# Modulation by direct fp32 products on four column tiles, and a new order of the first panels

## The chip, the cores and the metric

The kernel runs on one core of a Trainium2 chip. The metric is the device time of one execution in microseconds (us), from the first to the last instruction with what lies around them. Five engines work side by side and meet at semaphores: TensorE (PE), whose weight loads are listed as PEld, VectorE (DVE), ScalarE (ACT), GpSimd (POOL) and SyncE (SP), which here only issues DMA transfers.

## The reference, cut to what matters

Two transformer blocks run one after the other on 256 tokens of width 1024, in fp32. The change lies at the start of the first one:

```
mod = silu(c) @ w_ada + b_ada              # 1024 x 6144, in six parts: sh1, sc1, gt1, sh2, sc2, gt2
mod_c = silu(c_ctx) @ w_ada + b_ada        # the same for the context
h  = rmsnorm(x, g_norm1)   * (1 + sc1)  + sh1      # 256 x 1024
hc = rmsnorm(ctx, g_norm1) * (1 + scc1) + shc1     # 256 x 1024
cq, ckv, kpe, rq, rk, rv, rg       = split(h  @ w_in)   # 256 256 32 512 512 512 512 columns
_, ckv_c, kpe_c, _, rk_c, rv_c, _  = split(hc @ w_in)
q = rmsnorm(cq, g_q) @ w_uq                # latent attention's queries
... retention over rq, rk, rv with states from rk_c, rv_c, gated by silu(rg) ...
```

So nothing of `h` can be formed before sh1 and sc1 are there: the first 2048 columns of w_ada, 8 MB. The context needs only four of the seven panels of w_in.

## The kernel before, in words

**Units.** All weights come as units of 512 KB or less (128 partitions x 1024 fp32 values; mostly two slices of 128 rows of a panel of 512 columns). SP issues their DMAs in the order of one list, into six buffers `raw`, and waits before each for the release of the unit six places earlier. ACT then rounds a unit to `w_hi` (L1527), DVE forms the rest `w_lo` = raw - w_hi (L2093), into three buffers each, and PE makes a product as three in fp32r: hi x hi, lo x hi, hi x lo (`three`, L742 to L744). ACT may round a unit only when PE is through with the unit three places earlier.

**Names.** ada0 to ada3 are the first four panels of w_ada (shift: ada0, ada1; scale: ada2, ada3), each of four units. cq (two units of 4 slices), rq, ckvpe, rk, rv, rg (four units each) are panels of w_in, uq and ukv those of w_uq and w_ukv. Only ckvpe, rk and rv are multiplied with the context too. ada4 to ada11 are not PE's: DVE sums them itself from `raw` (L2060, L2066: "summed units", two instructions for each unit), and they stand in the list between other units as the table SUMS_BESIDE says.

**Order.** Each engine runs a list of its own that is written out by hand; nothing is reordered. `next(cq)` on PE is one unit of cq, `run(cq)` the rest. Transposes (`turn`, L884) of normalised rows go to a PSUM bank; ACT and DVE turn it into hT_hi and hT_lo (for x1 and ctx with gain and shift through `fbuf`; for mem, cq, ckv and ckvc by L1578/L1580 and L2157). `turn_before` makes a product wait for the pair of slices that it reads. The helper `feed_units(n)` on ACT and on DVE is what issues roundings and rests in the list's order; DVE's `feed_units(fed[0] + 1)`, ahead of the turn of mem among other places, issues exactly one more unit, whatever it is. `feed("rv")` issues up to two units past the last of rv, of which the second last buffer and the last become free only as rv's products end.

**ada0 to ada3 before.** `c_parts` holds silu(c) and silu(c_ctx) in four groups of 32 equal columns (hi and lo of each). Every slice takes two matmuls of 512 columns (L916, L917), with w_hi and w_lo. `ada_spread` (L946) takes the row of results back to columns, from which DVE makes shift and gain (L2198 to L2208). `keep_busy` (L754) are transposes of the identity with no use but to occupy PE.

Of the kernel before, what the change touches and what calls it, by code (L numbers as in the profile page):

```python
# [22 lines left out]
ALU = mybir.AluOpType  # L23
# [33 lines left out]
C_ONES = C_SEL + 2  # L57
# [16 lines left out]
def constants():  # L74
# [4 lines left out]
    c[[0, 32], C_SEL] = 1  # L79
    c[[64, 96], C_SEL + 1] = 1  # L80
# [46 lines left out]
for _g, _vs in enumerate(VEC_GROUPS):  # L127
    _at = 0
    for _name, _n in _vs:
# [7 lines left out]
SUMS_BESIDE = {**{(name, n): 1 for name in ("rv", "rg") for n in range(4)}, ("ukv1", 0): 14,  # L137
# [4 lines left out]
EARLIER = {"cq": (("cq", 0), ("rq", 0), ("rq", 1)),  # L142
           "wout2_0": (("wv1", 0), ("wv1", 1)),
           "wo0": (("wo0", 0), ("wo0", 1), ("wo1", 0))}


def plan_panels(a):
# [10 lines left out]
    def ada(ps):  # L158
        for p in ps:
            add(f"ada{p}", "sum" if p in SUMMED else "ada", a["w_ada"], 512 * p, 512)  # L160

    ada(range(4))
# [69 lines left out]
ADA_ORDER = [0, 1, 2, 3]  # L232


# [40 lines left out]
BUSY = {"score": 8, "start": 17, "spread": 8, "ada": 3,  "ffnpre": 14, "gu0": 8}  # L275
# [10 lines left out]
def build(nc, a, const, out):  # L286
    panels = plan_panels(a)
    units, units_of, summed = [], {name: [] for name, *_ in panels}, []

    def add_unit(name, k0, nk, cols, sources, kind):  # L290
        units_of[name].append(len(units))
        units.append((name, k0, nk, cols, sources))
        summed.append(kind == "sum")

    sums = [(name, k0, nk, cols, sources, kind) for p in SUMMED for name, kind, kt, nk, cols, sources in panels
            if name == f"ada{p}" for k0 in range(0, kt, nk)]
    for name, kind, kt, nk, cols, sources in panels:
        if kind == "sum":
            continue
        for other, n in EARLIER.get(name, ()):  # L300
            _, kind_, _, nk_, cols_, sources_ = next(x for x in panels if x[0] == other)
            add_unit(other, n * nk_, nk_, cols_, sources_, kind_)
        for n, k0 in enumerate(LATE_FIRST.get(name, range(0, kt, nk))):
            if any((name, n) in early for early in EARLIER.values()):
# [8 lines left out]
    split_units = [u for u in range(len(units)) if not summed[u]]  # L313
    split_of = {u: n for n, u in enumerate(split_units)}
    ends = set(last_unit.values())
    inner = np.cumsum([u not in ends and not summed[u] for u in range(len(units))]).tolist()
# [5 lines left out]
    with ExitStack() as ctx:  # L322
# [22 lines left out]
        c_parts = sb("c_parts", [P, KD, P], F32R)  # L345
        at[0] = c_parts_at
        late_sum = sb("late_sum", [P, 2, 512])
        assert at[0] == c_parts_at + 4 * KD * P
        csilu = sb("csilu", [P, 2, KD])
        modrow = sb("modrow", [P, 2, 512])  # L350
# [16 lines left out]
        cqT_hi = sb("cqT_hi", [P, 2, TOK], F32R)  # L367
        cqT_lo = sb("cqT_lo", [P, 2, TOK], F32R)
# [92 lines left out]
        junk = sb("junk", [P, D])  # L461
        fbuf = sb("fbuf", [P, 2, 2, TOK])
        k0 = sb("k0", [P, C_RCOS])
        ident = k0[:, C_ID:C_ID + P]
        sel_col = k0[:, C_SEL:C_SEL + 2]
# [63 lines left out]
        c_hi_ready = sem("c_hi_ready")  # L529
        c_lo_ready = sem("c_lo_ready")  # L530
# [90 lines left out]

        def gate_of(p):
            return gate[:, p // 8, 512 * (p % 2):512 * (p % 2) + 512]
# [87 lines left out]
        landed = {}  # L711

# [4 lines left out]
        def _(pe):  # L717
# [38 lines left out]
            def panel(name, outs, step, before=None):  # L756
# [6 lines left out]
                for u in units_of[name]:  # L763
                    if tail and u == tail[0]:
                        continue
                    if tail and u == tail[1]:
                        for v in tail:
                            pe.wait_ge(unit_ready, v + 1)
# [13 lines left out]
                    pe.wait_ge(unit_ready, u + 1)  # L782
# [70 lines left out]
            def turn(name, wait_src=None, pairs=None, banks=None):  # L853
# [8 lines left out]
                if name in UNSCALED:  # L862
                    ps_ = list(pairs or range(kt // 2))
                    for p in ps_:
                        claim(("turn", name, p), banks[p % 2] if banks else next_small())
# [12 lines left out]
                for p in pairs or range(kt // 2):  # L878
                    use = ("turn", name, p)
                    o = claim(use, banks[p % 2] if banks else next_small())  # L880
# [28 lines left out]
            turn_vectors(0)  # L909

            def ada_steps(p):
                name = f"ada{p}"
                use = (name, 0)

                def step(k, use, hi, lo, first, last):
                    pe.matmul(ps(use)[:, :], c_parts[:, k, :], hi, start=first, stop=False)  # L916
                    return pe.matmul(ps(use)[:, :], c_parts[:, k, :], lo, start=False, stop=last)  # L917

                yield from panel(name, [use], step)

            def ada(p):
                run(ada_steps(p))

            def sum_spread(p, b=None):
# [4 lines left out]
                pe.wait_ge(unit_ready, last_unit[f"ada{p}"] + 1)  # L929
# [7 lines left out]
            def ada_spread(p, b=None):  # L937

                use = ("spread", p)
                o = claim(use, next_small() if b is None else b)  # L940
                if p == 3:
                    keep_busy(o[:, P:2 * P], BUSY["spread"])
                emptied(pe, (f"ada{p}", 0))
                m = modrow[:, p % 2, :]
                for j in range(4):
                    ins = pe.matmul(o[:, 2 * j:2 * j + 2], m[:, j * P:(j + 1) * P], sel_col, start=True, stop=True)  # L946
                fill(ins, use)

            for p in range(4):
                claim((f"ada{p}", 0), p)  # L950
            keep_busy(ps(("ada3", 0))[:, 0:P], BUSY["start"])
            pe.wait_ge(c_lo_ready, 2)

            def chunk_unit(chunk):

                next(chunk)
                keep_busy(ps(("ada3", 0))[:, 0:P], BUSY["ada"])

            chunk = ada_steps(0)
            for _ in range(4):  # L960
                chunk_unit(chunk)
            run(chunk)
            chunk = ada_steps(1)
            chunk_unit(chunk)
            chunk_unit(chunk)
            turn_vectors(1)
            next(chunk)
            pe.wait_ge(in_sel, 16)
            ada_spread(0, 0)
            run(chunk)  # L970
            chunk = ada_steps(2)
            next(chunk)
            next(chunk)
            ada_spread(1, 1)
            next(chunk)
            turn("x1", None, range(2))
            run(chunk)
            chunk = ada_steps(3)
            next(chunk)
            turn("x1", None, range(2, 4))  # L980
            ada_spread(2, 2)
            run(chunk)
# [5 lines left out]
            ada_spread(3, 7)  # L988
            next(cq)
            next(rq)  # L990
            next(rq)
            run(cq)
            turn("ctx")
# [26 lines left out]
            rows_panel("uq0", cqT_hi, cqT_lo, turn_before("cq"))  # L1020

# [421 lines left out]
        def _(sp):  # L1443
            count = [0] * NRAW
            sp.dma_start(ident, const[:, C_ID:C_ID + P]).then_inc(in_ident, 16)
            for u, (name, k0, nk, cols, sources) in enumerate(units):
                slot = u % NRAW
                if u >= NRAW:

                    sp.wait_ge(unit_ready, u - NRAW + 1)  # L1450
                dst = unit_view(raw[slot], u).rearrange("p (k n) -> p k n", k=nk)
                for c0, width, matrix, m0 in sources:
                    src = matrix[k0 * P:(k0 + nk) * P, m0:m0 + width].rearrange("(k p) n -> p k n", p=P)
                    sp.dma_start(dst[:, :, c0:c0 + width], src).then_inc(raw_landed[slot], 16)
                    count[slot] += 16
                landed[u] = count[slot]
                for group, done, at_unit in ((1, in_vec, NRAW - 1), (2, in_conv, first_unit["rq"] + 2),
                                             (3, in_conv, first_unit["rq"] + 2)):
# [4 lines left out]
                for t in range(T):  # L1463
                    if u == (4, 6)[t]:
                        sp.dma_start(res[:, t, :], a["x"][t * P:(t + 1) * P, :]).then_inc(in_x[t], 16)
                if u == first_unit["rq"]:
# [20 lines left out]
        def _(pool):  # L1487
            pool.memset(mhalf[:, :], -0.5).then_inc(mhalf_ready, 1)
# [10 lines left out]
        def _(act):  # L1499
# [16 lines left out]
            def feed_units(stop):  # L1516

                while fed[0] < min(stop, len(units)):
                    u = fed[0]
                    fed[0] += 1  # L1520
                    if summed[u]:
# [8 lines left out]
            def feed_one(stop=None):  # L1530

                n = fed[0]
                while summed[n]:
# [73 lines left out]
            emptied(act, ("vec", 0))  # L1607
            act.activation(csilu[:, 0, :], vec("c"), ACT.Silu).then_inc(csilu_ready, 1)
# [1217 lines left out]
```

## Time and profile before

| | us |
|---|---|
| median of three executions | 848.87 (848.33 to 849.84) |
| profiled execution | 849.23 |
| its span | 847.4 |
| PE busy | 827.3 (98%) |
| PE weight loads busy | 721.5 (85%) |
| DVE busy | 588.7 (69%) |
| ACT busy | 467.9 (55%) |
| moved by DMA | 152.86 MB, 180 GB/s on average |

PE is busy nearly all the time, so the end moves with what PE has to do and with the time in which it waits. The averages hide the start: there the DMA queues are full and PE waits or runs transposes of no use. A row of a timeline reads: start, duration, engine, line, operation, output <- inputs, shapes, count, and in brackets the idle time of that engine just before and what ended it. Matmuls are pipelined: the shown duration of one is longer than the distance to the next, and a stretch of work is counted from start to start.

### The profile page before, as it was taken

The numbers are of one execution on the slowest core, as the hardware profiler recorded it, in microseconds if no ns is written. First come the engines' busy times: TensorE is split into PE (matmuls) and PEld (weight loads), VectorE is DVE, ScalarE is ACT, GpSimd is POOL, SyncE is SP. The second block draws the span as 40 slices with busy tenths as digits, with TensorE's granted clock in tenths as the row PEclk, the third lists the DMA queues.
The fourth block names the chain that finished last, engine by engine and source line by source line (L and its number), as shares of the span: only waits on it lengthen the run. The fifth ranks groups of instructions, "written<-read, shape, count | busy, mean of one in ns | idle before, by whom it ended". The sixth has DMA issues, their size and how long they took to land. (4 is left out here: it accounts for less than half of the span.)

```text
span 847.4 us, 12808 instructions
## 1 busy us (share of the span) xinstructions
PE 827.3 (98%) x4919; PEld 721.5 (85%) x4919; DVE 588.7 (69%) x919; ACT 467.9 (55%) x757; POOL 16.9 (2%) x24
## 2 busy tenths in 40 slices
PE   6999999999999999999999999999999999999996
PEld 5798888877899999988889978888978788888885
DVE  5885978788777777897767677577457655555444
ACT  6866364366356665663556684556545654444442
POOL 1001000000000000000000000010000000000000
PEclk9999999999999999999999999999999999999999
DMA  9973573165656656669758642254504656565551
GB/s 331 373 245 100 172 227 112 50 199 170 210 176 192 195 179 180 178 213 313 238 149 302 195 153 101 75 174 149 174 26 150 195 178 198 179 188 180 190 158 50
DMA packets 103668, 152.86 MB, mean 180 GB/s; under 512 B 6538, under 2 KB 55862, under 8 KB 103608
## 3 DMA queue, kind: packets, MB, share of 16 engines
q1 hardware_dynamic: 102296, 149.21, 55.6%
q10 hardware_dynamic: 1312, 2.83, 0.9%
q8 instruction: 39, 0.64, 0.3%
q14 instruction: 21, 0.17, 0.1%
HBM read 150.97 MB, written 1.05 MB: 179 GB/s over the span
## 5 line engine op out<-in xcount | busy, mean ns | idle before, releaser
L2093 DVE TENSOR_TENSOR w_lo<-raw,w_hi 128x1024 fp32r<-128x1024 f32 (+1 forms) x244 | 294.5, 1212 | 147.1 <-ACT w_hi L1527 146.2
L1527 ACT ACTIVATE w_hi<-raw 128x1024 fp32r<-128x1024 f32 (+1 forms) x244 | 254.5, 1050 | 197.4 <-PE bank L744 138.6
L742 PE MATMUL bank<-w_hi,hT_hi 128*128 128x512 f32 (+2 forms) x400 | 156.2, 390 | 1.2 <-DVE w_lo L2093 0.6
L744 PE MATMUL bank<-w_hi,hT_lo 128*128 128x512 f32 (+2 forms) x400 | 152.9, 382 | 0.0
L743 PE MATMUL bank<-w_lo,hT_hi 128*128 128x512 f32 (+2 forms) x400 | 152.7, 382 | 0.0
L845 PE MATMUL bank<-hT_hi,w_hi 128*128 128x256 f32 x512 | 145.1, 283 | 0.0
L847 PE MATMUL bank<-hT_hi,w_lo 128*128 128x256 f32 x512 | 145.0, 283 | 0.0
L846 PE MATMUL bank<-hT_lo,w_hi 128*128 128x256 f32 x512 | 145.0, 283 | 0.0
L846 PEld LDWEIGHTS bank<-hT_lo,w_hi 128*128 128x128 f32 x512 | 96.8, 189 | 0.0
L847 PEld LDWEIGHTS bank<-hT_hi,w_lo 128*128 128x128 f32 x512 | 96.8, 189 | 0.0
L845 PEld LDWEIGHTS bank<-hT_hi,w_hi 128*128 128x128 f32 x512 | 96.8, 189 | 0.0
L742 PEld LDWEIGHTS bank<-w_hi,hT_hi 128*128 128x128 f32 x400 | 75.2, 188 | 16.7 <-DVE w_lo L2093 2.3
L744 PEld LDWEIGHTS bank<-w_hi,hT_lo 128*128 128x128 f32 x400 | 75.1, 188 | 15.0
L743 PEld LDWEIGHTS bank<-w_lo,hT_hi 128*128 128x128 f32 x400 | 75.3, 188 | 13.4
L742 PE MATMUL bank<-w_hi,act_hi 128*128 128x512 f32 x176 | 69.7, 396 | 0.4 <-DVE w_lo L2093 0.3
L744 PE MATMUL bank<-w_hi,act_lo 128*128 128x512 f32 x176 | 68.5, 389 | 0.0
L743 PE MATMUL bank<-w_lo,act_hi 128*128 128x512 f32 x176 | 68.5, 389 | 0.0
L742 PEld LDWEIGHTS bank<-w_hi,act_hi 128*128 128x128 f32 x176 | 33.0, 188 | 8.5 <-DVE w_lo L2093 1.5
L743 PEld LDWEIGHTS bank<-w_lo,act_hi 128*128 128x128 f32 x176 | 33.0, 188 | 7.2 <-issue 0.5
L744 PEld LDWEIGHTS bank<-w_hi,act_lo 128*128 128x128 f32 x176 | 33.0, 188 | 7.0
L1495 POOL TENSOR_TENSOR rstd<-var,mhalf 128x2 f32<-128x2 f32 (+3 forms) x18 | 14.8, 823 | 825.1 <-DVE var L2752 254.7
L1143 PEld LDWEIGHTS bank<-k,prob 128*128 128x128 f32 x104 | 12.6, 140 | 14.7 <-ACT probT L1807 8.0
(346 smaller groups left out, 1196.6 us busy)
## 6 DMA issues: line engine op xcount, KB each, us to landing
raw<-w_up_dram SPq DMA_DIRECT2D x132, 256.0 KB, 3.4
raw<-w_ada_dram SPq DMA_DIRECT2D x48, 512.0 KB, 4.8
raw<-w_down_dram SPq DMA_DIRECT2D x44, 512.0 KB, 4.3
raw<-w_in_dram SPq DMA_DIRECT2D x40, 512.0 KB, 4.6
raw<-w_gate_dram SPq DMA_DIRECT2D x44, 256.0 KB, 2.9
raw<-w_out_dram SPq DMA_DIRECT2D x16, 512.0 KB, 3.4
raw<-wk_x_dram SPq DMA_DIRECT2D x8, 512.0 KB, 4.7
raw<-wv_x_dram SPq DMA_DIRECT2D x8, 512.0 KB, 3.4
```

Of the source, the lines that this page charges most:

```text
L742: pe.matmul(o, xh, yh, start=first, stop=False, skip_group_check=skip)
L743: pe.matmul(o, xh, yl, start=False, stop=False, skip_group_check=skip)
L744: return pe.matmul(o, xl, yh, start=False, stop=last, skip_group_check=skip)
L845: pe.matmul(o, hi[:, c:c + P], xh[:, k, :], start=f, stop=False, skip_group_check=True)
L846: pe.matmul(o, hi[:, c:c + P], xl[:, k, :], start=False, stop=False, skip_group_check=True)
L847: ins = pe.matmul(o, lo[:, c:c + P], xh[:, k, :], start=False, stop=last, skip_group_check=True)
L1143: ins = pe.transpose(o[:, j * P:(j + 1) * P], prob_of(i)[:, j * P:(j + 1) * P], ident)
L1495: pool.tensor_tensor(rstd[:, r, c:w], var[:, r, c:w], mhalf[:, c:w], ALU.pow).then_inc(rstd_ready, 1)
L1527: act.activation(unit_view(w_hi[n % NSPLIT], u), unit_view(raw[u % NRAW], u), ACT.Copy).then_inc(w_hi_ready, 1)
L2093: dve.tensor_tensor(unit_view(w_lo[n % NSPLIT], u), unit_view(raw[u % NRAW], u), unit_view(w_hi[n % NSPLIT], u).bitcast(F32), ALU.subtract ...
```

## The change

Four things change.

1. **ada0 to ada3 are multiplied directly from `raw`**, in plain fp32, with no rounding by ACT and no rest by DVE. `c_cols` holds silu(c) and silu(c_ctx) as two of 32 columns (the others are zero). A unit (2 slices x 512 columns) is four matmuls of 32 x 256, one for each slice and half, written to partitions 0, 32, 64 and 96 of a bank; `ada_spread` adds the slices (2 matmuls where there were 4).
2. **The list of units** begins ada0, ada2; then ada1 and ada3 stand among units of cq, rq and rg. x is loaded behind units 1 and 3, the context behind the third unit of rg.
3. **PE multiplies ten units of cq, rq and rg** with x before it turns to ckvpe, the first panel with the context; before there were six (cq, rq), and rg followed rv. The turn of cq stands ahead of the last unit of rv, and uq0 directly behind rv; ckv and ckvc are turned after uq0. silu(rg) is taken by ACT between the turns of the context, where the table that holds silu is still loaded.
4. **The summed units** stand beside rk 1 to 3, rv 0 to 3 and uq0, where they stood beside rv 0 to 3 and rg 0 to 3. `feed_units` on DVE is as it was.

```diff
-SUMS_BESIDE = {**{(name, n): 1 for name in ("rv", "rg") for n in range(4)}, ("ukv1", 0): 14,
+SUMS_BESIDE = {**{(name, n): 1 for name in ("rk", "rv") for n in range(4) if name == "rv" or n},
+               ("uq0", 0): 1, ("ukv1", 0): 14,
...
-EARLIER = {"cq": (("cq", 0), ("rq", 0), ("rq", 1)),
+EARLIER = {("ada1", 0): (("cq", 0),), ("ada1", 1): (("rq", 0),), ("ada1", 2): (("rq", 1),),
+           ("ada3", 2): (("rg", 0),), ("cq", 1): (("rg", 1), ("rq", 2), ("rg", 2)), ("rq", 3): (("rg", 3),),
...
-BUSY = {"score": 8, "start": 17, "spread": 8, "ada": 3,  "ffnpre": 14, "gu0": 8}
+BUSY = {"score": 8, "start": 24, "spread": 8, "ada": 4, "ffnpre": 14, "gu0": 8}
...
+            def direct_unit(u):
+                name, k0, nk, cols, _ = units[u]
+                use = (name, 0)
+                pe.wait_ge(raw_landed[u % NRAW], landed[u])
+                w = unit_view(raw[u % NRAW], u).rearrange("p (k n) -> p k n", k=nk)
+                for kk in range(nk):
+                    for half in range(2):
+                        j = 32 * (2 * kk + half)
+                        ins = pe.matmul(ps(use)[j:j + 32, 0:TOK], c_cols[:, k0 + kk, :],
+                                        w[:, kk, half * TOK:(half + 1) * TOK],
+                                        start=u == first_unit[name], stop=u == last_unit[name])
...
             next(cq)
+            direct_unit(units_of["ada1"][1])
             next(rq)
+            for u in units_of["ada1"][2:]:
+                direct_unit(u)
             next(rq)
+            ada_spread(1, 6)
+            for u in units_of["ada3"]:
+                direct_unit(u)
+            next(rg)
+            ada_spread(3, 6)
+            turn("x1", None, range(2, 3), (7,))
+            next(rg)
+            turn("x1", None, range(3, 4), (6,))
+            next(rq)
+            next(rg)
             run(cq)
-            turn("ctx")
+            run(rg)
+            turn("ctx", None, None, (6, 7, 0, 1))
             run(rq)
...
-            rows_panel("rv", hT_hi, hT_lo, None, cT, b=4)
-            rg = rows_steps("rg", hT_hi, hT_lo, b=2)
-            next(rg)
-            next(rg)
-            for name in ("cq", "ckv", "ckvc"):
-                turn(name)
-            run(rg)
+            rv = rows_steps("rv", hT_hi, hT_lo, None, cT, b=4)
+            for _ in range(3):
+                next(rv)
+            turn("cq", None, None, (0,))
+            run(rv)
+            rows_panel("uq0", cqT_hi, cqT_lo, turn_before("cq"))
+            turn("ckv", None, None, (2,))
+            turn("ckvc", None, None, (3,))
```

The three places below show what stands in a row on an engine (line numbers of the changed kernel differ by some ten).

DVE around the turn of mem, which PE makes behind the third of rk's four units. Before (memT_lo is what DVE makes of the turned rows, kpe_row the rows that it worked on ahead of it):

```order
L2242 TENSOR_TENSOR kpe_row<-rtmp 128x2x8
L2093 TENSOR_TENSOR w_lo_54<-raw_137,w_hi_51 128x1024
L2157 SCALAR_TENSOR_TENSOR memT_lo<-bank,vcol_145,memT_hi 128x256 x8
L2093 TENSOR_TENSOR w_lo_52<-raw_132,w_hi_49 128x1024
L2066 SCALAR_TENSOR_TENSOR modrow<-raw_133,csilu,gate 128x512
```

The same place now:

```order
L2244 TENSOR_TENSOR kpe_row<-rtmp 128x2x8
L2069 SCALAR_TENSOR_TENSOR modrow<-raw_134,csilu,modrow 128x512 x2
L2168 SCALAR_TENSOR_TENSOR memT_lo<-bank,vcol_145,memT_hi 128x256 x8
L2104 TENSOR_TENSOR w_lo_54<-raw_135,w_hi_51 128x1024
L2069 SCALAR_TENSOR_TENSOR modrow<-raw_130,csilu,modrow 128x512 x2
```

The unit that `feed_units(fed[0] + 1)` issues ahead of the turn was the rest of rk's fourth unit; now it is a summed unit, and the rest of rk's fourth unit follows behind memT_lo.

ACT at the end of rv. Before (the last row with w_hi_49 is the unit that waits for the end of rv's products):

```order
L1527 ACTIVATE w_hi_49<-raw_132 128x1024
L1705 ACTIVATE rv_row<-bank 128x512 x2
L1705 ACTIVATE rvc_row<-bank 128x512 x2
L1708 ACTIVATE decay<-decay 128x512 x4
L1527 ACTIVATE w_hi_50<-raw_134 128x1024
L1715 ACTIVATE xi_f<-k_63,lgam 128x256
```

The same place now:

```order
L1539 ACTIVATE w_hi_51<-raw_135 128x768
L1539 ACTIVATE w_hi_49<-raw_130 128x1024
L1590 ACTIVATE cqT_hi<-bank,vcol_145 128x256
L1592 ACTIVATE cqT_hi<-bank,vcol_145 128x256
L1723 ACTIVATE rv_row<-bank 128x512 x2
L1723 ACTIVATE rvc_row<-bank 128x512 x2
L1726 ACTIVATE decay<-decay 128x512 x4
L1590 ACTIVATE ckvT_hi<-bank,vcol_145 128x256
```

cqT_hi stands now directly behind the rounding that waits for rv's end (it is a unit of ukv0); on DVE the rest of that unit stands ahead of cqT_lo likewise.

PE from the last unit of ada2 to the first product with x, now (raw_131 is ada2's last unit, raw_133 ada1's first):

```order
L894 MATMUL bank<-k_143,row 128x128 x4
L928 MATMUL bank<-raw_131,c_cols 32x256 x4
L894 MATMUL bank<-k_143,row 128x128 x4
L955 MATMUL bank<-k_143,modrow 128x4 x2
L764 MATMUL bank<-k_143 128x128 x8
L928 MATMUL bank<-raw_133,c_cols 32x256 x4
L764 MATMUL bank<-k_143 128x128 x8
L752 MATMUL bank<-w_hi_49,hT_hi 128x256
```

Before, all sixteen units of ada0 to ada3 stood ahead of the first product with x; now nine do.

## Rows read from the trace of the kernel before

**Rows 1.** The page's slices 1 to 40: granted clock (tenths), PE busy.

```profile
PE   6999999999999999999999999999999999999996
PEclk9999999999999999999999999999999999999999
```

**Rows 2.** Windows: length, busy of PE PEld DVE ACT POOL, clock, DMA share, GB/s.

```profile
30.00:40.00 10.00, 10.00 (x70) 8.71 (x69) 8.45 (x16) 8.12 (x12) 0.00 (x0) 1.00 1.02 371
24.00:26.00 2.00, 1.84 (x5) 1.28 (x5) 1.93 (x5) 1.69 (x3) 0.00 (x0) 0.50 1.05 387
26.00:28.00 2.00, 2.00 (x13) 1.81 (x12) 1.48 (x4) 1.06 (x1) 0.00 (x0) 0.85 1.00 365
```

**Rows 3.** Timeline of the start: ada1's last unit lands, a wait, to the first product.

```profile
18.28 1.06 ACT L1527 ACTIVATE w_hi<-raw 128x1024 fp32r<-128x1024 f32 x1 [0.97 <-DMA raw<-w_ada_dram]
22.63 0.51 PE L916 MATMUL bank<-w_hi,c_parts 128*128 128x512 f32 x1 [0.79 <-DVE w_lo L2093]
33.57 1.02 ACT L1597 ACTIVATE fbuf<-bank,modc,acol 128x256 f32<-128x256 f32 x2 [0.81 <-DVE acol L2208]
35.57 1.23 DVE L2093 TENSOR_TENSOR w_lo<-raw,w_hi 128x1024 fp32r<-128x1024 f32 x1
37.64 0.36 PE L742 MATMUL bank<-w_hi,hT_hi 128*128 128x256 f32 x1
```

**Rows 4.** Timeline of PE: a unit of cq, one of rg, plain fp32, start of ckvpe.

```profile
46.39 0.28 PE L742 MATMUL bank<-w_hi,hT_hi 128*128 128x256 f32 x1
49.27 1.91 PE L884 MATMUL bank<-k,in_ctx 128*128 128x128 f32 x16
56.59 0.38 PE L742 MATMUL bank<-w_hi,hT_hi 128*128 128x288 f32 x1
114.81 0.39 PE L742 MATMUL bank<-w_hi,hT_hi 128*128 128x512 f32 x1
117.53 0.39 PE L742 MATMUL bank<-w_hi,hT_hi 128*128 128x512 f32 x1
135.35 3.62 PE L1041 MATMUL bank<-rqT,rkT 128*128 128x256 f32 x16
```

**Rows 5.** Timeline of ACT: ckvpe's first rounding, behind the turn of ctx; silu(rg).

```profile
52.30 0.68 ACT L1527 ACTIVATE w_hi<-raw 128x576 fp32r<-128x576 f32 x1
131.16 1.08 ACT L1730 ACTIVATE sgate<-bank 128x512 f32<-128x512 f32 x2
```

**Rows 6.** Timeline at the turn of mem.

```profile
86.06 1.23 DVE L2093 TENSOR_TENSOR w_lo<-raw,w_hi 128x1024 fp32r<-128x1024 f32 x1
87.40 3.23 DVE L2157 SCALAR_TENSOR_TENSOR memT_lo<-bank,vcol,memT_hi 128x256 fp32r<-128x256 f32 x8
87.50 0.48 PE L742 MATMUL bank<-w_hi,hT_hi 128*128 128x512 f32 x1
```

**Rows 7.** Timeline behind rv: ACT, DVE, then PE to the states.

```profile
115.07 1.06 ACT L1527 ACTIVATE w_hi<-raw 128x1024 fp32r<-128x1024 f32 x1 [4.38 <-PE bank L744]
116.16 1.23 DVE L2093 TENSOR_TENSOR w_lo<-raw,w_hi 128x1024 fp32r<-128x1024 f32 x1 [1.26 <-ACT w_hi L1527]
117.94 2.21 ACT L1708 ACTIVATE decay<-decay 128x512 f32<-128x512 f32 x4
124.17 0.47 ACT L1578 ACTIVATE cqT_hi<-bank,vcol 128x256 fp32r<-128x256 f32 x1
125.03 0.87 DVE L2157 SCALAR_TENSOR_TENSOR cqT_lo<-bank,vcol,cqT_hi 128x256 fp32r<-128x256 f32 x2 [1.10 <-ACT cqT_hi L1580]
130.94 1.28 DVE L2354 COPY rkT<-bank 128x512 f32<-128x512 f32 x2
129.27 0.41 PE L742 MATMUL bank<-w_hi,cqT_hi 128*128 128x384 f32 x1 [0.32 <-DVE w_lo L2093]
131.67 0.60 PE L1030 MATMUL bank<-rvc_row,rkf 128*128 128x128 f32 x3
```

**Rows 8.** Timeline of PE: its longest wait behind the start.

```profile
503.08 0.33 PE L1143 MATMUL bank<-k,prob 128*128 128x128 f32 x1 [1.46 <-ACT probT L1807]
```

More of the change, by code:

```diff
@@ L159, in ada @@
         for p in ps:
-            add(f"ada{p}", "sum" if p in SUMMED else "ada", a["w_ada"], 512 * p, 512)
-    ada(range(4))
+            add(f"ada{p}", "sum" if p in SUMMED else "direct", a["w_ada"], 512 * p, 512)
+    ada((0, 2, 1, 3))
     add("cq", "rows", a["w_in"], 0, 256, nk=4)
@@ L287, in build @@
     panels = plan_panels(a)
-    units, units_of, summed = [], {name: [] for name, *_ in panels}, []
+    units, units_of, summed, direct = [], {name: [] for name, *_ in panels}, [], []
     def add_unit(name, k0, nk, cols, sources, kind):
@@ L947, in ada_spread @@
                 fill(ins, use)
[L949 to L964, printed above, removed]
@@ L965, in _ @@
-            chunk_unit(chunk)
-            turn_vectors(1)
-            next(chunk)
-            pe.wait_ge(in_sel, 16)
[L969 to L980, printed above, removed]
+            turn_vectors(0, 4)
@@ new lines, in _ @@
+            for p, b in ((0, 0), (2, 1), (1, 6), (3, 7)):
+                claim((f"ada{p}", 0), b)
+            idle = ps(("ada3", 0))[:, 0:P]
+            keep_busy(idle, BUSY["start"])
+            pe.wait_ge(csilu_ready, 3)
+            for u in units_of["ada0"]:
+                direct_unit(u)
+                keep_busy(idle, BUSY["ada"])
+            turn_vectors(1, 2)
+            pe.wait_ge(in_sel, 16)
+            ada_spread(0, 3)
+            for u in units_of["ada2"][:3]:
+                direct_unit(u)
+                keep_busy(idle, BUSY["ada"])
@@ L981, in _ @@
+            turn("x1", None, range(1), (4,))
+            direct_unit(last_unit["ada2"])
+            turn("x1", None, range(1, 2), (5,))
             ada_spread(2, 2)
-            run(chunk)
+            keep_busy(idle, BUSY["spread"])
+            direct_unit(units_of["ada1"][0])
+            keep_busy(idle, BUSY["spread"])
             cT = (hcT_hi, hcT_lo)
@@ L1448, in _ @@
                 if u >= NRAW:
-                    sp.wait_ge(unit_ready, u - NRAW + 1)
+                    v = u - NRAW
+                    if not direct[v]:
+                        sp.wait_ge(unit_ready, by_dve[v])
+                    elif v in ends:
+                        ready(sp, (units[v][0], 0))
+                    else:
+                        sp.wait_ge(direct_used, inner_direct[v])
                 dst = unit_view(raw[slot], u).rearrange("p (k n) -> p k n", k=nk)
@@ L1532, in feed_one @@
                 n = fed[0]
-                while summed[n]:
+                while summed[n] or direct[n]:
                     n += 1
@@ L1659, in _ @@
             turn("ctx", None, range(2))
-            feed_units(last_unit["rq"] + 2)
+            for t in range(T):
+                use = ("rg", t)
+                ready(act, use)
+                free(act.activation(sgate[:, t, :], ps(use)[:, :], ACT.Silu), use)
+            feed_units(first_unit["ckvpe"] + 1)
             full("ctx", 3)
```

224 lines of the change are left out of this document (105 added, 119 removed).

## The prediction

> **What bounds the kernel now.** I read the slices of the page first: PE is 90% busy or more in all but the first and the last [rows 1], so a change pays only by what it takes from PE or from PE's waits. Then the windows of the start: the DMA queues are full (share about 1.0, 371 to 387 GB/s), while VectorE (DVE) and ScalarE (ACT) are busy 8 tenths of the time with halves of weights [rows 2]. Then the timeline: w_ada's eighth unit, the tenth transfer of 512 KB, is rounded the moment it lands, at 18.28 us, but the first product with x starts only at 37.64 [rows 3]. Until then PE does nothing but modulation, transposes and filler. From there to the attention it hardly waits. So the start is worth up to 15 us, and each new wait behind it costs its full length. Last I read, at the places that the order of instructions names, what PE does at each moment and who releases it [rows 4 to 8].
>
> **The change part by part.** All sums are made in the profiled execution's time, 849.23 us (span 847.4); the median shown is 0.36 lower, and I take that off at the end.
>
> *The start.* With 387 GB/s [rows 2] a unit of 512 KB lands every 1.35 us. In the new list ada2's last unit is again the tenth such transfer: 18.25. Its product, ACT's copy, the spread and the gain are worth some 2.1 us. Before, the chain from the gain's first user on ACT (33.57) to the first product (37.64) took 4.1 us [rows 3], of which about 1 us was hT_lo waiting behind a weight's rest on DVE (35.57, 1.23 us); 3.0 to 3.5 are left, so the first product starts at about 23.4, 14 us earlier. But seven units of ada1 and ada3 are still to come. The last one is the 22nd transfer, 12 behind the tenth: 18.25 + 12 x 1.35 = 34.5. PE's way there: one unit of cq (46.39 to 49.27: 2.88 us), two of rq (114.81 to 117.53: 2.72 each [rows 4]), a spread, and six direct units: 23.4 + 8.7 + six direct units, 33.5 to 34.5 if one takes 0.2 to 0.4. So DMA sets this point.
>
> What a direct unit costs no row shows. From above: a plain fp32 product of 256 columns takes (3.62 - 0.38)/15 = 0.216 us start to start [rows 4], where 0.38 is the pipelined duration of the last; four in a row 0.86. From below: all four at once, 0.22. I take 0.4 (two by two), since the four write to different partitions and have no operand in common but c_cols; at anything up to that the sum stays with DMA. The Trainium skill (TensorE: Matmul & The Clock Gate, Part 3: Packing small matmuls) says that matmuls whose outputs lie at partitions 32j run concurrently; no row here shows it, and by that rule the unit would be 0.2 to 0.3 and the time below the same within 0.2 us.
>
> So ada3 is through at 35.0. Behind it PE has six units of rg and rq (16.3), one of cq (2.9), a spread and two short turns (1.3), the turn of ctx (49.27 to 50.93, 1.7) and two vector transposes (0.1): ckvpe could start at 57.3. Before it started at 56.59 [rows 4], with rg's four units (10.9) still ahead: like with like, 67.5. Gain 10.2.
>
> *Waits in it.* rq's third unit waits about 0.6 for DVE, which makes spread, gain and hT_lo of pair 2 first. At the turn of ctx ACT rounded ckvpe's first unit 3.0 us behind the turn's start, at 52.30, and PE needed it at 56.59. Now ACT takes silu(rg) first, 1.08 [rows 5], and only one unit of rq (2.72) instead of two covers: w_lo comes at turn + 5.5, PE is there at turn + 4.7. (Rounding 0.68, its rest about as much.) With the same delay once more at ckvpe's second unit, and a bit at the fourth, 1.7. The start is left with 10.2 - 0.6 - 1.7 = 7.9.
>
> *The turn of mem.* DVE's helper issues one unit ahead of it. That was rk's fourth rest, made in 86.06 to 87.29, just in time for PE's 87.50 [rows 6]. Now that unit is a summed one, and the rest comes behind memT_lo. The summed unit ends at about 87.6; memT_lo takes 3.23, or until 90.9; the rest 1.23: 92.1. PE, through with its transposes at 87.5, waits **4.6 us**. Nothing covers it: everything on PE is queued behind this product. DVE reaches the place no sooner than before, since decay and k_pe ahead of it hang on the end of ckvpe, as PE's own three units of rk do.
>
> *The query latent.* Its transposes lie inside rv, but on ACT cqT_hi is queued behind the rounding that waits for rv's last product: 115.07 in the trace, and DVE's rest of that unit is 116.16 to 117.39 [rows 7]. cqT_hi takes 0.86 (124.17 to 125.03), so it is ready by 117.0; cqT_lo then goes to 117.4 + 0.87 = 118.2. uq0 could have started at 114.81: **3.4 us**. Before, rg's units lay there. After uq0 (2.4) come 24 transposes (2.6) to 123.3, and the retention's states need a bank that DVE frees with rkT. ACT does the copies of rv and exp(decay) first (some 4.1 us: before, from the rounding's end to 117.94 + 2.21), then ckvT_hi, DVE ckvT_lo and the copy: 124.3. **1.0 us** more. The wait of 0.32 before uq0 goes [rows 7]. Sum 4.1.
>
> *Hidden at nothing:* 16 roundings and 16 rests less in the first 35 us, where DMA bounds; and the summed units, which lie beside products of rk and rv. Should DVE lose its lead there, a product of rv would wait for its rest, by the length of one summed unit.
>
> *Sum:* 849.2 - 7.9 + 4.6 + 4.1 = 850.0.
>
> *The clock.* After short waits on PE, the last of 0.79 us before 22.63 [rows 3], the granted clock fell to half (0.50 in 24 to 26, 0.85 in 26 to 28) and stayed there for some 3.2 us [rows 2]: half of that, 1.6 us, is what one fall costs. Waits of 4.6 and 3.4 us in one piece are longer than any behind the start of the trace, where the longest is 1.46 [rows 8]. Bounds: nothing, or 2 x 1.6. I take 1.6 for the first, 0.8 for the second. The Trainium skill (same page, Why this matters for your kernels) warns of idle gaps between bursts as what throws the clock back; the row agrees in kind. 852.4 in this execution's time, or **852.0** as a median.
>
> **The rivals.**
> - *The clock holds* in both waits. For it: the wait of 1.46 left it at full speed [rows 1, 8]. Then 850.0 - 0.4 = 849.6, no change that can be told. The bound here is 0.2%, 1.7 us, about what this measurement can tell.
> - *Faster: ACT and DVE keep ahead.* Their lists lost 16 units of work, and the small waits that I sum to 3.3 (0.6, 1.7, 1.0) hang on them being late by about a us. If they are early there and the clock holds, 849.6 - 3.3 = 846.3. It decides where the small waits fall under 0.9 us together. Against it: each hangs on an event on PE (end of a turn, end of rv), not on backlog.
> - *The four column tiles run one after the other.* 0.86 a unit. Then PE and not DMA paces ada0 and ada2: with four filler transposes (0.5) a unit it is through with ada2 at 21.5 instead of 18.7, first product 26.6; the path to ada3's end is 26.6 + 8.7 + 7 x 0.86 = 41.3, 6.3 later than 35.0. 858. For it: the only fp32 rows. Against it: separate partitions.
> - *SP holds the transfers back.* Three DMAs of ada1 and ada3 now wait for DVE's rest of cq and rq units, which wait for the modulation. I find them issued at 23 to 27, some 3 us ahead of their turn. If the queue runs dry for 2 us, all behind it moves by as much: 854.
>
> **How the numbers follow.** Forecast 0.45 (850.8 to 854), clock holds 0.22, faster rival 0.12, tiles in a row 0.13, transfers held back 0.08. The 80% range takes in the clock's case and the held transfers and part of the slow tiles: 847.5 to 857. Faster by over 0.2%: 0.12. Within 0.2% (847.2 to 850.6): the clock's case and the lower edge of the forecast, 0.25. Slower: 0.63.
>
> **What would show it.** The first L752 product near 23.4, and the last L928 near 35.0; w_ada's units landing every 1.35 us. ckvpe's first product at 59 to 60. Then one idle time of some 4.6 us on PE at rk's fourth unit, released by DVE w_lo, and one of 3.4 at uq0, released by DVE cqT_lo, with a granted clock of 0.5 behind them or not. L928 four by four: starts 0.2 apart would mean tiles in a row. I am wrong if the wait at rk's fourth unit is under 2 us, or if the first product comes later than 27.

## The result

The changed kernel takes 854.82 us (median of 4, 853.94 to 856.74) against 848.81 us: ratio 1.0072, 95% interval 1.0051 to 1.0094. The forecast was 852.0 with a range of 847.5 to 857.0: the side and the range hold, the size is 2.8 us short. The same kernel run again for an experiment gave 856.92 us (median of 4), ratio 1.0097 (1.0081 to 1.0114); all eight executions together have a median of 856.2. So the time of the changed kernel is known to about 2 us, and differences to its 854.82 below are no more certain than that. The profiled execution is the fastest of its four, 853.94; in its terms the forecast was 852.4.

What TensorE (PE) waits for in the changed kernel, the first seven rows (in total, times, longest; all us). The load of c's columns ahead of the first product (vrow) and the waits for probT in the attention were there before too, 5.2 and 2.3 in all. Against the others the kernel before had nothing above 1.46 us behind its start [rows 8]:

```profile
PE bank L752 <- DVE w_lo L2104: 5.7, 5, 4.3
PE bank L917 <- DMA vrow<-c_ctx_dram: 3.7, 1, 3.7
PE bank L752 <- DVE cqT_lo L2168: 3.3, 1, 3.3
PE bank L1153 <- ACT probT L1816: 2.3, 3, 1.5
PE bank L917 <- DVE fbuf L2157: 1.8, 1, 1.8
PE bank L928 <- DMA raw<-w_ada_dram: 1.3, 2, 1.1
PE bank L1040 <- DVE rkT L2354: 1.1, 1, 1.1
```

Two of them are the forecast's waits (4.3 at rk's fourth unit, 3.3 at uq0), one is its small one behind (1.1). The wait of 1.8 for fbuf it did not have in this form: it lies ahead of two small transposes of parameter vectors (88 x 88, L917) that PE makes just before ckvpe, and is called the vectors' wait below. PE's timeline at those places; columns: start, duration, instruction, idle time before it and who ended it. The first three answer to [rows 3, 4]:

```profile
23.74 0.36 PE L752 MATMUL bank<-w_hi,hT_hi 128*128 128x256 f32 x1 [0.32 <-DVE hT_lo L2165]
34.63 1.93 PE L928 MATMUL bank<-raw,c_cols 128*32 128x256 f32 x32
36.50 0.50 PE L752 MATMUL bank<-w_hi,hT_hi 128*128 128x512 f32 x1
...
61.91 0.37 PE L917 MATMUL bank<-k,vrow 88*128 88x88 f32 x2 [1.76 <-DVE fbuf L2157]
...
97.76 0.79 PE L752 MATMUL bank<-w_hi,hT_hi 128*128 128x512 f32 x1 [4.28 <-DVE w_lo L2104]
...
131.31 0.41 PE L752 MATMUL bank<-w_hi,cqT_hi 128*128 128x384 f32 x1 [3.35 <-DVE cqT_lo L2168]
137.36 0.82 PE L1040 MATMUL bank<-rvc_row,rkf 128*128 128x128 f32 x5 [1.10 <-DVE rkT L2354]
```

The first product with x starts at 23.74 (forecast 23.4), ada3 is through at 36.50 (35.0), ckvpe starts at 62.35 (59.6). The last row, the retention's states, lay at 131.67 before [rows 7]: 5.69 us later now. The distance stays: the last output transfer is issued at 849.00 us where it was at 843.29, 5.71 later. The two profiled spans differ by 4.7 only because the span ends 4.1 us behind that issue before and 3.1 now, at a place that the change does not touch.

The turn of mem on VectorE (DVE), answering to [rows 6]: the summed unit, then memT_lo, and only then the low part of rk's fourth unit:

```profile
91.89 1.54 DVE L2069 SCALAR_TENSOR_TENSOR modrow<-raw,csilu,modrow 128x512 f32<-128x512 f32 x2
93.35 3.22 DVE L2168 SCALAR_TENSOR_TENSOR memT_lo<-bank,vcol,memT_hi 128x256 fp32r<-128x256 f32 x8
96.49 1.22 DVE L2104 TENSOR_TENSOR w_lo<-raw,w_hi 128x1024 fp32r<-128x1024 f32 x1
```

In the page's slices of the whole span (PE busy and granted clock, in tenths; 21.3 us each) the three waits show against the row of before [rows 1]: PE is at 8, 7 and 7 tenths in slices 3, 5 and 7 (the vectors', rk's and uq0's), and the clock is lower in slice 5:

```profile
PE   7989797999999999999999999999999999999997
PEclk9999899999999999999999999999999999999999
```

The windows at rk's wait show it closer (length, busy of PE, PEld, DVE, ACT, POOL, then the granted clock, DMA share, GB/s). The clock falls while PE still waits and is low behind it:

```profile
90.00:100.00 10.00, 5.72 (x29) 4.75 (x28) 9.66 (x23) 4.91 (x10) 0.00 (x0) 0.78 0.28 75
100.00:110.00 10.00, 10.00 (x40) 8.12 (x39) 7.45 (x11) 1.06 (x1) 0.00 (x0) 0.87 0.85 290
```

### The profile page after: what moved, and what is told of

Same layout as the page of the kernel before. It is cut to its first block and busy times, and to the rows that moved or that the text cites. A ratio compares the mean times of both kernels' runs of the same rounds, so it can differ in the third digit from the quotient of the medians.

```text
span 852.1 us, 12903 instructions
## 1 busy us (share of the span) xinstructions
PE 824.0 (97%) x4992; PEld 714.5 (84%) x4992; DVE 569.5 (67%) x900; ACT 448.5 (53%) x739; POOL 17.1 (2%) x25
## 5 line engine op out<-in xcount | busy, mean ns | idle before, releaser
L2104 DVE TENSOR_TENSOR w_lo<-raw,w_hi 128x1024 fp32r<-128x1024 f32 (+1 forms) x228 | 275.3, 1212 | 148.5 <-ACT w_hi L1539 147.7
L1539 ACT ACTIVATE w_hi<-raw 128x1024 fp32r<-128x1024 f32 (+1 forms) x228 | 238.2, 1050 | 206.1 <-PE bank L754 145.4
L752 PE MATMUL bank<-w_hi,hT_hi 128*128 128x512 f32 (+2 forms) x400 | 158.0, 395 | 6.4 <-DVE w_lo L2104 5.4
```

The source lines that it names most:

```text
L752: pe.matmul(o, xh, yh, start=first, stop=False, skip_group_check=skip)
L1539: act.activation(unit_view(w_hi[n % NSPLIT], u), unit_view(raw[u % NRAW], u), ACT.Copy).then_inc(w_hi_ready, 1)
L2104: dve.tensor_tensor(unit_view(w_lo[n % NSPLIT], u), unit_view(raw[u % NRAW], u), unit_view(w_hi[n % NSPLIT], u).bitcast(F32), ALU.subtract ...
```

## The experiments

One table first: where the profiled execution of each kernel starts the first product with x, ckvpe and the states, at which waits the clock fell to half (0.50), and the median. "Vectors'", "rk's" and "uq0's" are the three waits of the result.

| kernel | x | ckvpe | states | half clock at | median us | ratio to before |
|---|---|---|---|---|---|---|
| before | 37.64 | 56.59 | 131.67 | (in the start) | 848.5 | |
| changed | 23.74 | 62.35 | 137.36 | rk's wait | 854.82 | 1.0072 |
| e7, the same | 23.85 | 62.78 | 140.35 | rk's, uq0's | 856.92 | 1.0097 |
| e1 | 24.57 | 63.07 | 135.48 | vectors', uq0's | 851.31 | 1.0031 (1.0019 to 1.0042) |
| e2 | 24.08 | 63.60 | 136.30 | vectors', rk's | 854.16 | 1.0067 (1.0054 to 1.0080) |
| e3 | 24.23 | 64.06 | 131.03 | vectors' | 848.62 | 0.9998 (0.9989 to 1.0006) |
| e4 | 23.87 | 63.03 | 138.93 | vectors', uq0's | 855.19 | 1.0082 (1.0069 to 1.0095) |
| e6 | 27.29 | 69.04 | 143.43 | rk's | 860.09 (one run) | |
| e8 | 23.77 | 60.14 | 135.22 | a wait at 39 us | 851.90 | 1.0041 (1.0029 to 1.0054) |
| e5 | 24.40 | 61.17 | 126.80 | none | 844.72 | 0.9960 (0.9948 to 0.9973) |
| e9 | 25.06 | 62.85 | 126.84 | none | 842.19 | 0.9925 (0.9913 to 0.9938) |
| e10 | 24.53 | 62.34 | 126.38 | none | 841.44 | 0.9918 (0.9904 to 0.9931) |

(ckvpe of before and of e8 has rg's four units, 10.9 us, still behind it; 56.59 is 67.5 like for like.)

**e1_sum_moved.** Is it the order on DVE that makes the wait at rk's fourth unit?

```
-SUMS_BESIDE = {**{(name, n): 1 for name in ("rk", "rv") for n in range(4) if name == "rv" or n},
+SUMS_BESIDE = {("rk", 1): 2, ("rk", 3): 1, **{("rv", n): 1 for n in range(4)},
```

> The changed kernel with one of its summed units standing two places earlier (two beside rk's second unit, none beside its third), so that what VectorE does just ahead of the turn of mem is the low part of rk's fourth unit again. Theory: the 4.28 us wait at rk's fourth unit goes, and with it the half clock behind it (2.2 us): 854.8 - 4.3 - 2.2 = 848.3 us, the clock 1.0 from 96 to 103. Rival: VectorE is the engine that is late in this stretch whatever its order (the 1.54 us of the summed unit only moves), so the wait moves to rk's third unit or stays at 1.5 to 3 us: 851 to 853. Rival: it was the transfer of rk's fourth unit, which would be as late as before: 854.8.

Its first waits behind the load of c:

```profile
PE bank L752 <- DVE cqT_lo L2168: 3.3, 1, 3.3
PE bank L917 <- DVE fbuf L2157: 1.8, 1, 1.8
PE bank L752 <- DVE hT_lo L2165: 0.9, 1, 0.9
PE bank L1040 <- DVE rkT L2354: 0.8, 1, 0.8
PE bank L752 <- DVE w_lo L2104: 0.6, 1, 0.6
```

(These are the waits up to 170 us.) The 4.3 is gone, and what is left on w_lo is a wait of the start: the rivals of a late DVE and of a late transfer fall. The time came 3.5 us down from 854.82 (5.6 from the second measurement, 856.92), not 6.5. The profile says why: two other waits that the clock had survived in the changed kernel's first profile were now followed by half clock. ckvpe's first unit behind the vectors' transposes took 4.78 us instead of 3.26, and uq0 3.98 instead of 2.17. Its start is also 0.7 us later (ckvpe at 63.07).

**e2_cq_first.** Is uq0's wait the order on ScalarE (ACT) and DVE, cqT behind a unit of ukv0 whose rounding waits for rv's end? In the changed kernel:

```profile
128.06 1.06 ACT L1539 ACTIVATE w_hi<-raw 128x1024 fp32r<-128x1024 f32 x1 [5.07 <-PE bank L754]
129.15 1.23 DVE L2104 TENSOR_TENSOR w_lo<-raw,w_hi 128x1024 fp32r<-128x1024 f32 x1 [5.14 <-ACT w_hi L1539]
130.29 0.87 DVE L2168 SCALAR_TENSOR_TENSOR cqT_lo<-bank,vcol,cqT_hi 128x256 fp32r<-128x256 f32 x2
```

The edit in short:

```
 ACT:  -feed("rv"); turn("cq")          +feed("rv", 1); turn("cq"); feed("rv")
 ACT:  -exp(decay); turn("ckv"), ("ckvc")   +turn("ckv"), ("ckvc"); exp(decay)
 DVE:  -feed("rv"); turn("cq")          +feed("rv", 1); turn("cq"); feed("rv")
```

> The changed kernel with the turn of cq on ScalarE and VectorE ahead of the rounding of ukv0's first unit, and the exponential of the decay behind the turns of ckv and ckvc. Theory: the 3.35 us wait at uq0's first product falls to 0.5 or less, and the 1.1 us wait for the bank of rk's turned rows grows by 0 to 1: -3.0, 851.8 us. Rival: the wait is for VectorE, which still does the low part of rv's fourth unit and a summed unit there, and cq's turned tiles only come 1 us sooner: 853.8. Rival: the later wait takes all of it (the bank of rk's turned rows 1.1 to 4): 854.5.

uq0 follows rv without a gap (129.96). The edit moves the turn of cq on both engines; that the order on one of them alone would have made the wait, or how much of it, no run shows. Behind uq0 the wait for rkT grew to 1.46 and one for rqT, 1.01, is new:

```profile
PE bank L1040 <- DVE rkT L2356: 1.5, 1, 1.5
PE bank L1051 <- ACT rqT L1738: 1.0, 1, 1.0
```

So 3.35 went and 1.4 came back; a start that is 1.3 later (ckvpe at 63.60) and the half clock behind the vectors' wait, 1.5, hide the rest. The theory of the wait holds, the expected 851.8 was missed by 2.4.

**e3_both.** Both edits.

> Both edits: the summed unit moved and cq's turn ahead of ukv0. Theory (the two waits are independent terms of the sum): 854.8 - 6.5 - 3.0 = 845.3 us; what stays against the kernel before (848.8) is then the net of the start, -3.5 to -5. Rival: what one wait gives back is lost in the other, as VectorE has the same work in both stretches: 848 to 850. Rival: the earlier start is itself worth nothing to the end: 848.8 or more.

848.62, the kernel before's time, 3.3 above the expected 845.3. Both waits are gone (states at 131.03); what I had left out is the 1.0 for rqT, the half clock behind the vectors' wait (ckvpe's first unit 4.79 us, 3.26 at full clock: 1.5 us), and a start that is 1.7 later in this profile (ckvpe at 64.06 against 62.35). The two edits alone gave 3.5 and 0.7 us, together 6.2.

**e4_filler.** Does idleness make the half clock?

```
             turn("mem")
+            busy = ("busy", "mem")
+            o = claim(busy, place[("turn", "mem", 0)][0])
+            keep_busy(o[:, 0:P], 26)     # and two more, which fill and free the bank
             run(rk)
```

> The changed kernel with 28 transposes of the identity in TensorE's idle time ahead of rk's fourth unit, in a bank that the turn of mem has given back; the wait for VectorE stays. Theory: the half clock behind the wait comes from TensorE's idleness; kept busy from about 94.2 it stays at 1.0, rk's fourth unit is as quick as in the kernel before (2.8 us for its first half in place of 5.05), and the time is 854.8 - 2.2 = 852.6 us. Rival: the half clock comes from elsewhere, and the fillers change nothing (854.8) or run beyond the wait at half speed and cost up to 2 us (856.8). If 0.7 us of idleness is enough for the fall, the fillers run at half clock and the result lies at 854.8 to 856.

```profile
96.49 3.06 PE L764 MATMUL bank<-k 128*128 128x128 f32 x26 [0.79 <-DVE memT_lo L2173]
99.39 0.27 PE L1017 MATMUL bank<-k 128*128 128x128 f32 x1
99.50 0.27 PE L1018 MATMUL bank<-k 128*128 128x128 f32 x1
99.97 0.50 PE L752 MATMUL bank<-w_hi,hT_hi 128*128 128x512 f32 x1 [0.20 <-DVE w_lo L2109]
```

Locally yes: 0.79 us of idleness and then fillers left the clock at 1.0, and rk's fourth unit took 2.88 us for its first half where the changed kernel took 5.05 (97.76 to 102.81) and before 2.83. That is 2.2 us. The time, 855.19 where 852.6 was expected, did not follow, because half clock came behind the vectors (1.5) and at uq0 (1.6) instead: 0.7 later start + 1.5 - 2.2 + 1.6 = 1.6, and the states do lie 1.57 later than in the changed kernel.

**e7_same_again.** The changed kernel, unedited. Which waits does the clock fall at a second time?

> The changed kernel itself a second time, for what differs from one execution to the next. Theory: which of its waits are followed by half clock is not fixed (in the first profile the one at rk's fourth unit, in the profiles of the variants the one at the vectors' turn or at uq0 too), so this profile shows one to three such stretches and the times lie between 853.5 and 857.5 with a median of 854.5 to 855.5. Rival: in this kernel it is always the wait at rk's fourth unit alone: the profile shows just that one, from 96 to 103 us, and the time is 854 to 855.

```profile
98.20 0.79 PE L752 MATMUL bank<-w_hi,hT_hi 128*128 128x512 f32 x1 [4.27 <-DVE w_lo L2104]
98.79 0.63 PE L753 MATMUL bank<-w_lo,hT_hi 128*128 128x512 f32 x1
...
103.49 0.42 PE L752 MATMUL bank<-w_hi,hcT_hi 128*128 128x512 f32 x1
...
132.02 0.66 PE L752 MATMUL bank<-w_hi,cqT_hi 128*128 128x384 f32 x1 [3.34 <-DVE cqT_lo L2168]
...
136.00 1.85 PE L894 MATMUL bank<-k,ckv_row 128*128 128x128 f32 x8
```

The same waits to 0.02 us, but this time uq0 runs at half clock as well (0.32 between starts; 132.02 to 136.00 is 3.98 us, 2.17 in the first profile). That, the transposes behind it (1.69 to the next start, 0.87 before) and a start 0.4 later make the states 3.0 us later. So one and the same wait, uq0's, is sometimes followed by half clock and sometimes not. Over the seven profiles that have them (changed, e1 to e4, e6, e7) the vectors' wait of 1.8 us was followed by it 4 times in 7, uq0's of 3.3 in 3 of 5, rk's of 4.3 in 4 of 4. What it cost, in time of the work behind it, was 1.5 at each vectors' wait; 1.6 (e2, e6), 2.2 and 2.5 at rk's; 1.6 (e4) and 2.6 (e1, e7, with the transposes behind uq0) at uq0's.

**e6_two_tiles.** What do the four column tiles give?

```
-                        j = 32 * (2 * kk + half)
+                        j = 32 * half      # the copy and the spread read 64 rows
```

> The changed kernel with its direct units on two column tiles in place of four (each tile takes both of the unit's 128-row slices, one after the other). If the four tiles work side by side and the 0.47 us of a unit that has landed comes from that, two tiles need about twice as long a unit (0.8 to 0.95 us), 16 units cost 5 us more of TensorE time and the start up to 3 us: 856 to 858. If no more than two tiles overlap at a time, or what sets the 0.47 us is the issue of eight passes at 0.06 us each, a unit stays at 0.45 to 0.55 us and the time at 854 to 855.5. If nothing overlaps it stays too.

Four direct units of ada3 in a row, two tiles (the changed kernel's row is above, 34.63, 1.93 us):

```profile
39.59 3.65 PE L928 MATMUL bank<-raw,c_cols 128*32 128x256 f32 x32
43.17 0.50 PE L752 MATMUL bank<-w_hi,hT_hi 128*128 128x512 f32 x1
```

(43.17 - 39.59)/4 = 0.90 us a unit, against (36.50 - 34.63)/4 = 0.47: four tiles halve the unit, so their products overlap. The first product came at 27.29. The one execution took 860.09, 5.3 us above 854.82 and 3.2 above e7's median, which was measured beside it; 856 to 858 was expected.

**e8_direct_alone.** The direct modulation without the moved panel (of the list of units; PE, ACT and DVE follow it): rg, the summed units and the turns of cq, ckv and ckvc stand where they stood before; cq and rq alone are in front.

```
-EARLIER = {("ada1", 0): (("cq", 0),), ("ada1", 1): (("rq", 0),), ("ada1", 2): (("rq", 1),),
-           ("ada3", 2): (("rg", 0),), ("cq", 1): (("rg", 1), ("rq", 2), ("rg", 2)), ...
+EARLIER = {("ada1", 0): (("cq", 0),), ("ada1", 1): (("rq", 0),),
```

> The direct fp32 modulation alone: rg's panel stands behind rv as in the kernel before, with the summed units beside rv and rg and the turns of cq, ckv and ckvc inside rg; six units (cq, rq) stand ahead of the context's products. Theory: the start's gain is the direct modulation's and stays (ckvpe at 50.5 to 53 us in place of 56.6, 4 to 6 us), the waits at rk's fourth unit and at uq0 are the moved panel's and go: 848.8 - 4 to 6 = 843 to 845 us. Rival: without rg's units the start has nothing to cover the transfers and the turn of x1, and TensorE waits there: ckvpe at 54 to 56, 846.5 to 849. Rival: the wait at rk's fourth unit comes with the earlier start whatever stands in the front, as the transfers and VectorE don't move with it: 848 to 852.

```profile
PE bank L750 <- DVE w_lo L2098: 4.7, 6, 3.3
...
PE bank L750 <- DVE hT_lo L2159: 3.1, 3, 2.1
...
PE bank L892 <- DVE in_ctx L2129: 1.3, 1, 1.3
PE bank L953 <- ACT modrow L1631: 1.2, 2, 0.6
```

Ahead of 55 us lie 3.6 of the 4.7 for w_lo and all of the rest; at uq0 w_lo has 0.3 as before, and at rk there is no wait. ckvpe starts at 60.14, 3.5 us later than before, and the time is 3.7 us up. So the waits at rk and uq0 belong to the moved panel, but so does the gain: without rg's units too little covers ada1, ada3 and the second half of x's turn. In this front order, which is mine, at least; the one of before might wait less.

**e5_ctx_cover.** e3, and the third wait taken away: the vectors' transposes claim banks 0 and 1, which hold ctx's last pairs until DVE has them in fbuf, the last thing ahead of ckvpe.

```
 PE:   -turn_vectors(2), (3); ckvpe     +ckvpe's first unit; turn_vectors(2), (3); the rest
 ACT:  -silu(rg); round ckvpe's first   +round ckvpe's first; silu(rg)
```

> The kernel with both edits (summed unit moved, cq's turn ahead of ukv0) and a third: the two transposes of vectors, which want the banks of the turn of ctx, stand behind ckvpe's first unit in place of ahead of it, and ScalarE rounds that unit ahead of rg's two silu. Theory: the 1.79 us wait at the turn of the vectors goes (ckvpe starts 0.2 to 0.5 us behind rq's end), and with it the half clock that followed it in four of the five profiles so far (1.6 us): 848.6 - 1.8 - 1.6 = 845.2 us, between 844.5 and 847. Rival: what ckvpe then waits for (the third pair of ctx, rounded later, or the bank that silu gives back) takes the 1.8 us in another place: 848 to 849. Rival: VectorE's chain to the turn of mem is bound by itself and not by TensorE: 847.5 to 848.6.

```profile
61.17 0.37 PE L752 MATMUL bank<-w_hi,hT_hi 128*128 128x288 f32 x1 [0.19 <-ACT sgate L1679]
```

0.19 us in place of 1.8, and no half clock: 844.72, as expected (845.2), 3.9 below e3. Some of that is not the edit's: e5's profile was 0.9 us ahead of e3's at ada3's end already (37.48 against 38.35).

**e9_rows_first.** e5, with rkT's copies on DVE ahead of ckvT_lo, and rqT's on ACT ahead of the exponentials.

> The kernel with the three edits so far, and behind cq's turn VectorE copies rk's turned rows ahead of ckv's low parts, and ScalarE rq's turned rows ahead of the exponentials. Theory: the 1.46 us wait for the bank of rk's turned rows and the 1.01 us wait for rq's turned rows go, 844.7 - 2.5 = 842.3 us. Rival: what is moved behind (ckv's low parts, the decay's exponential) becomes the next wait, at the decay's product or at ukv0: 843.5 to 844.7.

842.19, 2.5 below e5 as expected, and the states follow uq0 and the 24 transposes at once. Nothing came back.

**e10_less_filler.** `BUSY["ada"]` from 4 to 3.

> The same with three filler transposes in place of four behind each of the direct units of ada0 and ada2 (0.13 us each, 8 units of which 7 stand ahead of ada2's last), so that TensorE is through ada2 about 0.9 us sooner. Theory: the front of the kernel is bound by transfers by now: ada3's last units wait as much longer for theirs (0.3 to 1.2 us in place of 0 to 0.7), the end of ada3 moves by 0.3 us or less, and the time stays within 0.4 us of the kernel without this edit. Rival: TensorE's own work sets ada3's end, as it did in the changed kernel's first profile, and the whole 0.7 to 0.9 us is gained. Rival: with fewer fillers the clock falls in the first 20 us and 1 to 2 us are lost.

841.44, 0.75 below e9. Its interval overlaps e9's, and its profile shows no wait for w_ada in the front where e9's shows two:

```profile
35.95 1.07 PE L928 MATMUL bank<-raw,c_cols 128*32 128x256 f32 x16
37.31 0.64 PE L928 MATMUL bank<-raw,c_cols 128*32 128x256 f32 x8 [0.29 <-DMA raw<-w_ada_dram]
38.63 0.64 PE L928 MATMUL bank<-raw,c_cols 128*32 128x256 f32 x8 [0.68 <-DMA raw<-w_ada_dram]
```

(e9.) Neither theory is settled by it. It is the fastest version of the study: 0.8% under the kernel before, 1.6% under the changed one.

## Why the prediction was right in kind and short in size

At the retention's states, first profile against before:

| step | forecast us | measured us |
|---|---|---|
| start, with its small waits | -7.9 | -5.1 (67.46 to 62.35) |
| wait at rk's fourth unit | +4.6 | +4.28 |
| half clock behind it | +1.6 | +2.2 (elsewhere 1.6 or 2.5; 0 with fillers, e4) |
| wait at uq0 | +3.4 | +3.35 |
| half clock behind it | +0.8 | 0; in e7 2.6 |
| bank freed by rkT, less 0.32 | +0.7 | +0.8 |
| sum | +3.2 | +5.5 (5.69 read off) |

*Right.* The mechanism, its places and its two prices. Both waits were read from the order of instructions on DVE and ACT and sized by rows of before, and each goes with the edit that takes its cause away (e1, e2). The first product was 0.3 us off, which was partly luck: in the first profile c's columns came earliest of all (PE starts at 3.73), and the first product came at 23.74 to 25.06 over the nine profiles with these direct units in this order.

*The step that failed is the start's gain*, the term of 10.2 less 2.3, by 2.8 us. It has three parts.
- ada3's end: 36.5, not 35.0, in the first profile and 37.1 to 39.2 in the eight others that keep its direct units, their tiles and their order. I had the transfers set it, at 34.5, with PE there at 33.5 to 34.5. In the first profile PE's own work set it: between the first product and ada3's end PE waited for nothing. The seven direct units took 3.45 us, not 2.8 (0.57 where one stands alone, 0.50 each for two, 0.47 for four in a row, where I had 0.4), the units of cq and rq with the spread 9.3, not 8.7, and the first product was 0.3 late. The transfers were not faster: they did not keep 387 GB/s but moved 354 and 287 in the windows below. SyncE (SP) issued w_ada's last two units at 28.14 and 31.0; it had waited 2.5 us for the second one's slot, which a direct unit on PE gave back, and 3.7 and 2.0 us ahead of earlier ones for slots that DVE's rests (w_lo) gave back. So the rival of held transfers was partly true, inside the likeliest case: PE and DMA arrive close together here, and in five of the other profiles PE waited 0.3 to 1.0 us for w_ada on this way.

```profile
24.00:28.00 4.00, 4.00 (x35) 3.37 (x35) 2.53 (x3) 1.39 (x2) 0.00 (x0) 1.00 1.05 387
28.00:32.00 4.00, 4.00 (x30) 2.62 (x29) 0.12 (x1) 0.38 (x1) 0.00 (x0) 1.00 1.02 354
32.00:36.00 4.00, 4.00 (x43) 3.04 (x45) 1.26 (x3) 1.06 (x1) 0.00 (x0) 1.00 0.87 287
28.14 3.23 SPq L1468 DMA_DIRECT2D raw<-w_ada_dram  x2
```

- At the turn of ctx I had 1.7 us for late weights. It was about 2.4, and its main part another wait, 1.76: the banks of the vectors' transposes. The late rest of ckvpe's first unit was there as I had it (ready at 60.95, 5.5 behind the turn's start at 55.48) but lay inside the longer wait; at ckvpe's later units PE waited for nothing. The diff gives the turn of ctx the banks 6, 7, 0, 1, and the next two claims are 0 and 1. I had looked at what each product reads, not at what it writes.
- The remaining half us is the products themselves: the six units of rg and rq behind ada3 took 17.0 us, not 16.3. A unit behind a spread, a turn or another panel took 2.84 to 2.90 (0.31 to 0.34 from its first product to the second), and only one that followed its own panel 2.72, the figure that I had used for all.

*The clock* was priced too low: I had 1.6 at rk (2.2), and nothing for the vectors' wait, which I did not know. In the first profile half clock cost 2.2, in e7 some 4.8; that is 2.6 of the 3.0 us between these two executions. The other six of the changed kernel have no profile, but the mean granted clocks of all eight go the same way: 0.995 to 0.997 in the four of 853.94 to 855.55, 0.992 or 0.993 in the four of 856.74 to 858.33. Before's 18 runs of one comparison lie within 2.0 us. The Trainium skill (TensorE: Matmul & The Clock Gate, Why this matters for your kernels) warns of idle gaps. The traces agree in that the clock fell at all four waits of 4.3 us and not at the one that e4 filled; uq0's 3.35 us in the first profile, with the clock at 1.0 behind it, show that a gap need not have that effect. The rival "the clock holds" (849.6) never happened at rk's wait.

*Tiles.* The rival of tiles in a row is out: 0.47 for four, 0.90 for two. With two tiles (e6) the kernel comes close to what that rival had worked out (first product 26.6, measured 27.29; 858, measured 860.1), since its unit costs what I had given there, 0.86. The Trainium skill (TensorE: Matmul & The Clock Gate, Part 3: Packing small matmuls) has such products run concurrently; the trace agrees in kind. My estimate of 0.2 to 0.3 us from it was not reached. I had worked that from plain products of 0.216 us. In e6 two products on one tile, beside two on the other, take 0.90: 0.45 each if the two tiles overlap, and then four tiles overlap fully. But 0.90 is also four times 0.22, what four plain products take one after the other; then two tiles would not overlap at all, and four only in part. Which of the two holds no run here tells.

*ACT and DVE ahead*, the faster rival: the small waits that it needed under 0.9 together were 0.6, 2.4 and 1.1 (the second mostly for a bank).

Where did the gain of the start go, then? Into waits that the new front does not need. The two edits of e3 give back 6.2 us and reach before's time; e5 and e9 take away the vectors' wait and the two behind uq0, and what is left is 0.75% faster than before. 62.85 against 67.46 at ckvpe is 4.6 us of e9's 6.0.

## What to carry to other kernels

When a unit of work is put into a helper's list "one ahead", look at what that helper now does at each place that calls it: a summed unit in the slot of a needed one cost 4.3 us with no more work on any engine. After a change of banks follow each bank to its next claim, whatever that product reads. And count a wait on TensorE at more than its length: here 1.5 to 2.6 us on top, in 11 of the 16 waits of 1.8 to 4.3 us, so that ordering it away is worth more than its row in the waits says. Filling it with idle transposes kept the clock at that place (2.2 us), but e4 shows no gain in the whole time from it.

## What the runs showed of the hardware

- Four fp32 products with 32 rows of output each, 256 columns, in four column tiles: 0.47 us together; on two tiles 0.90. A plain fp32 product of 256 columns took 0.216 before [rows 4].
- Granted clock: full (1.00, the 2.4 GHz level) through an idle time of 0.79 us followed by transposes (e4) and behind one of 2.1 us (e8, at 47.02), half (0.50, the 1.2 GHz level) behind idle times of 4.27 and 4.28 us in all four profiles that have them, and behind one of 3.34 us in e8 (at 38.96). Ahead of uq0, behind 3.3 us, it was half in one execution of the changed kernel and full in the other; behind 1.8 us it was full in both of these and in e6, and half in e1 to e4, which make the same products up to there. At half clock rk's products start 0.43 us apart in place of 0.23 and uq0's 0.32 in place of 0.18, and the transposes behind uq0 slow down too (1.69 to the next start in place of 0.87, e7).
- The load of c's columns let PE start between 3.73 and 5.04 us after the span's start in executions of the changed kernel and its variants: up to 1.3 us that no edit made. How much of it reaches the end no run tells.
